# A two-layer mixture-of-experts network: permanent routing tables, fewer routing products, and fetches moved into the last expert block

## The chip, the cores and the metric

The kernel runs on one core of one Trainium2 chip. The metric is the device time of one execution in microseconds; the kernel before has a median of 3048.8 us over 3 runs (3047.92 to 3056.55). Its five engines are named as the profile names them: PE (TensorE, matmuls; PEld its weight loads), DVE (VectorE), ACT (ScalarE), POOL (GpSimd) and SP (SyncE, which here only issues transfers).

## The reference, cut to what matters

512 tokens of width 1024 in float32 pass a first network of two layers and then a second one of two layers. Each layer of the first network is a mixer (a gated delta rule in layer 0, a sparse attention in layer 1) with a layer norm behind it, and a mixture of experts with a layer norm behind it:

```python
h = layer_norm(DEEPNORM_ALPHA * h + mix, ln_mix_g[layer], ln_mix_b[layer])
ffn = hier_moe(h, ...)     # per token: best of 4 groups, best 2 of its 4 experts
h = layer_norm(DEEPNORM_ALPHA * h + ffn, ln_ffn_g[layer], ln_ffn_b[layer])
# hier_moe: logits of 4 groups and of 16 experts; y = sum of 2 weighted
#           expert outputs (silu(x @ wg) * (x @ wu)) @ wd, hidden width 256
```

The change concerns only what lies between a mixer's output projection and the first projection of what follows, once in each of the two layers.

## The kernel before, in words

**Arithmetic.** A matrix product in float32 is done as three products of rounded parts: x and w are each split into a high part (ACT copies with rounding) and a low part (DVE or POOL subtracts), and PE adds high x high, low x high and high x low. In the code `wf` is a weight tile as loaded, `wh` its high part, `wl` its low part. Tokens are in four tiles of 128 (`TT = 4`), the width in eight slices of 128 (`KT = 8`, `HALF = 4`).

**Stages.** The program is a row of stages. At the end of each (`Stage.__exit__`, L72) semaphores are cleared and all engines meet in a barrier, so nothing crosses it that is not issued by hand in an earlier stage. Each engine has its own order of work, written out in the code; a wait holds all that stands behind it on that engine. Four stages matter here, in this order, in each layer:

1. *Output norm* (`stage_out_norm`, tiles `gwo_...` in layer 0 and `nwo_...` in layer 1). PE computes the second half of the output projection tile by tile (L1082), between them the routing logits of an earlier tile (`Logits.pe`, L1118: per tile 8 slices x 3 products of 20 columns) and the transposes of the normed tile (`Turn.pe`, L964). ACT and DVE split the transposed tile (L970, L975), and the logits of a tile wait for that (`lo_done`). At the end DVE adds the bias (`Logits.take`, L1124). `LayerNorm` works on DVE: statistics, `centre` (L1004) with the gain, `finish` (L1016) with the shift; the root between them is on ACT.
2. *Experts* (`stage_experts`, tiles `exp_...` and `rt_...`). SP first loads four small constant tables (`Route.load`: descending numbers, thresholds, places, a counter `iota_b`), then a counter of 256 columns (L1473), then the weights of blocks 0 and 1 (L1395, L1400). DVE works out from the logits which expert and which slot each token gets (`Route.slots`), waiting for all four tables behind its second step; PE counts the tokens per expert in between (`Route.pe`, four accumulating products of 16 columns at L1298; in the trace each is two instructions). Tokens are thus sorted into blocks of 128 per expert. PE gathers the tokens of a pair of blocks by a product with a 0/1 matrix (`choose` on DVE L1627, L1633 builds it; L1511), multiplies with the gate and up weights (L1527, `body`), transposes the hidden tile (L1537) and multiplies with the down weights (L1548); DVE multiplies the two hidden halves (`hid`, L1653), ACT does the silu and copies y, SP stores each block's y to memory (L1479). `pairs` runs blocks 0 and 1, then a hardware loop from a number read from a table (`last_pair`, L1449), then the last pair. Here both layers have 16 blocks. DVE splits half of each block's low parts, POOL the other half (L1414). Ahead of `pairs` DVE computes the mixing weights (`Route.weights`) and scales the four tiles of h (L1674). When the last y is stored, POOL fetches for each tile of tokens the rows of its two experts by index (L1614, into expert weight tiles that are free by then, `rows_back`), and DVE adds them to h (L1685).
3. *Norm behind the experts* (`stage_ffn_norm`, tiles `ffn_ln_...`). SP loads gain and shift (L991, L992), in layer 1 also the gain of the second network's norm, then the first weights of the next projection; ACT and POOL split the first half of them in this stage (`hi_first` at t = 1, L153; `lo_first`, L159). DVE norms tile by tile, PE transposes, ACT and DVE split.
4. The next projection, in layer 0 behind a short stage that builds bias tables.

Where a line number is a helper's (L153, L159, L964), the tile's name tells the stage.

## Time and profile before

| | |
|---|---|
| median of 3 runs | 3048.8 us (3047.92 to 3056.55) |
| the profiled execution, its own time | 3048.18 us |
| its span in the profile | 3046.4 us |
| PE busy | 2520.5 us (83% of the span) |
| DVE, ACT, POOL busy | 1244.7, 970.6, 756.1 us |
| mean granted clock of PE | 0.898 |
| transfers | 304.42 MB, 100 GB/s in the mean |

How to read it: the profile is of one execution. The time outside the span is 1.8 us. Times in rows are counted from the span's start. A timeline row gives start, duration, engine, line, operation, written tile <- read tiles, shapes and the number of merged instructions; in brackets the idle time of the engine before it and what ended it. A row of a window gives its length, then busy time (number of instructions) of PE, PEld, DVE, ACT and POOL, the granted clock of PE as a share of 2.4 GHz (1.00 is the upper of its two levels, 0.50 the lower), the busy share of the 16 DMA engines and GB/s. Busy shares say little by themselves: what counts is which wait ends last in each stage.

### The profile page before, as it was taken

The page shows a single profiled execution, that of the slowest core. Times are in us where ns is not written, and L with a number is a line of the kernel's source. Part 1 is how long each engine was busy: PE and PEld are TensorE (multiplying, and loading weights), DVE is VectorE, ACT ScalarE, POOL GpSimd, SP SyncE. Part 2 cuts the span into 40 slices and gives each one's busy share as a digit, 9 for nine tenths or more (in the row PEclk, how much of TensorE's full clock was granted, in tenths as well). Part 3 has the DMA queues.
Part 4 walks back from the last instruction along what each step waited for, and adds up shares of the span by engine and source line. Part 5 has one row for each costly group of instructions (what it writes and reads, how often), then busy time and mean ns, then how long its engine had stood idle before and what let it go on. Part 6 is the DMA issues. An engine that isn't in the chain of part 4 may idle for free. (4 is left out here: it accounts for less than half of the span.)

```text
span 3046.4 us, 34677 instructions
## 1 busy us (share of the span) xinstructions
PE 2520.5 (83%) x13130; PEld 1983.7 (65%) x13130; DVE 1244.7 (41%) x2600; ACT 970.6 (32%) x1543; POOL 756.1 (25%) x214
## 2 busy tenths in 40 slices
PE   6996888687992987997998378986999878896998
PEld 4774777576771775666775346765887737675886
DVE  3524555435444306765543544142022262222122
ACT  2332112223441114762443224242222332332222
POOL 2430000212441320010333211323443202234441
PEclk9997999888995996997999688997999989997999
DMA  4350000016873233112686411212322202223221
GB/s 111 102 208 7 1 1 1 28 53 209 282 260 115 85 85 134 50 56 85 209 278 204 160 36 52 88 56 70 127 97 78 87 28 69 71 70 100 97 83 63
DMA packets 220925, 304.42 MB, mean 100 GB/s; under 512 B 52226, under 2 KB 139796, under 8 KB 220772
## 3 DMA queue, kind: packets, MB, share of 16 engines
q1 hardware_dynamic: 218484, 294.18, 29.6%
q0 software_dynamic: 2304, 8.39, 0.8%
q8 instruction: 89, 1.46, 0.2%
q14 instruction: 48, 0.39, 0.0%
HBM read 270.97 MB, written 31.56 MB: 99 GB/s over the span
## 5 line engine op out<-in xcount | busy, mean ns | idle before, releaser
L159 POOL TENSOR_TENSOR branch_weights_wl<-branch_weights_wf,branch_weights_wh 128x2048 fp32r<-128x2048 f32 (+1 forms) x66 | 300.0, 4546 | 779.3 <-ACT branch_weights_wh L153 779.3
L1414 POOL TENSOR_TENSOR rt_wl<-rt_wf,rt_wh 128x2048 fp32r<-128x2048 f32 x32 | 167.1, 5223 | 396.9 <-ACT rt_wh L1410 256.3
L153 ACT ACTIVATE branch_weights_wh<-branch_weights_wf 128x2048 fp32r<-128x2048 f32 (+1 forms) x66 | 125.0, 1894 | 411.5 <-PE bprojc_acc L201 129.2
L201 PE MATMUL merge_acc<-xh,branch_weights_wh 128*128 128x512 f32 x384 | 151.1, 393 | 18.3 <-PEq L72 18.3
L201 PE MATMUL merge_acc<-xl,branch_weights_wh 128*128 128x512 f32 x384 | 150.7, 393 | 0.0
L201 PE MATMUL merge_acc<-xh,branch_weights_wl 128*128 128x512 f32 x384 | 150.5, 392 | 0.0
L159 POOL TENSOR_TENSOR nsa_weights_wl<-nsa_weights_wf,nsa_weights_wh 128x2048 fp32r<-128x2048 f32 x13 | 59.8, 4604 | 295.7 <-ACT nsa_weights_wh L153 295.7
L1410 ACT ACTIVATE rt_wh<-rt_wf 128x2048 fp32r<-128x2048 f32 x64 | 122.0, 1907 | 3.8 <-DMA rt_wf<-moe_w_up 3.8
L1548 PE MATMUL exp_ps_y<-rt_wf,exp_ht 128*128 128x512 f32 x256 | 117.7, 603 | 3.7 <-ACT exp_ht L1589 3.7
L1527 PE MATMUL exp_ps_gu<-rt_wh,exp_xh 128*128 128x512 f32 x256 | 113.2, 442 | 0.0
L159 POOL TENSOR_TENSOR in_weights_wl<-in_weights_wf,in_weights_wh 128x2048 fp32r<-128x2048 f32 x16 | 75.0, 4686 | 127.1 <-ACT in_weights_wh L153 109.5
L201 PE MATMUL gproj_acc<-xh,in_weights_wh 128*128 128x512 f32 x256 | 100.4, 392 | 4.2 <-POOL in_weights_wl L159 4.2
L2707 DVE TENSOR_TENSOR merge_prod<-merge_gate,merge_b 128x512 f32<-128x512 f32 x32 | 21.9, 684 | 196.8 <-PE merge_b L2651 196.8
L1527 PE MATMUL exp_ps_gu<-rt_wl,exp_xh 128*128 128x512 f32 x256 | 100.9, 394 | 0.0
L1527 PE MATMUL exp_ps_gu<-rt_wh,exp_xl 128*128 128x512 f32 x256 | 100.9, 394 | 0.0
L201 PE MATMUL gproj_acc<-xh,in_weights_wl 128*128 128x512 f32 x256 | 99.7, 389 | 0.0
L201 PE MATMUL gproj_acc<-xl,in_weights_wh 128*128 128x512 f32 x256 | 99.6, 389 | 0.0
L201 PEld LDWEIGHTS merge_acc<-xh,branch_weights_wh 128*128 128x128 f32 x384 | 73.0, 190 | 33.9 <-issue 18.7
L1511 PE MATMUL exp_ps_xh<-exp_pick,xh 128*128 128x256 f32 x512 | 78.6, 299 | 15.5 <-DVE exp_pick L1633 12.3
L1643 DVE CAST exp_xl<-exp_ps_xl 128x1024 fp32r<-128x1024 f32 x32 | 39.2, 1224 | 127.0 <-PE exp_ps_gu L1527 103.9
L625 PE MATMUL gchunk_ps<-gchunk_tm,gchunk_m 128*128 128x128 f32 x384 | 61.5, 312 | 32.7 <-DVE gchunk_m L749 32.7
L805 POOL MEMSET gscan_state<- 128x1024 f32 x1 | 1.0, 951 | 334.7 <-POOLq L72 334.7
(598 smaller groups left out, 6529.6 us busy)
## 6 DMA issues: line engine op xcount, KB each, us to landing
branch_weights_wf<-w_in SPq DMA_DIRECT2D x56, 1024.0 KB, 4.9
rt_wf<-moe_w_gate SPq DMA_DIRECT2D x64, 512.0 KB, 6.6
rt_wf<-moe_w_up SPq DMA_DIRECT2D x64, 512.0 KB, 7.7
rt_wf<-moe_w_down SPq DMA_DIRECT2D x32, 1024.0 KB, 6.0
in_weights_wf<-gdn_w_in SPq DMA_DIRECT2D x16, 1024.0 KB, 5.5
moe_rows<-exp_y SPq DMA_DIRECT2D x32, 512.0 KB, 3.0
moe_rows<-gproj_zeros SPq DMA_DIRECT2D x1, 12288.0 KB, 35.5
merge_bwf<-w_branch SPq DMA_DIRECT2D x12, 1024.0 KB, 5.0
```

The costliest lines, as they stand in the source:

```text
L153: act.activation(self.h[u][:, :, 0:self.cols(b)], self.s.f[u][:, :, 0:self.cols(b)], ACT.Copy).then_inc(self.s.hi_ready, 1)
L159: pool.tensor_tensor(self.l[u][:, :, 0:self.cols(b)], self.s.f[u][:, :, 0:self.cols(b)], self.h[u][:, :, 0:self.cols(b)].bitcast(F32), ALU ...
L201: mm = pe.matmul(self.acc[:, s, 0:cols], lhs[:, P * s:P * s + P], rhs, start=(u == 0 and k == 0 and n == 0), stop=(u == 1 and k == HALF - ...
L625: mm = pe.matmul(bank(i, 3, c), b["m"][:, c, :], b["tm"][:, c, :], start=True, stop=True)
L805: pool.memset(state[:], 0.0).then_inc(zeroed, 1)
L1410: act.activation(self.h[b][u][:], self.f[b][u][:], ACT.Copy).then_inc(self.hi_ready[u], 1)
L1414: eng.tensor_tensor(self.l[b][u][:], self.f[b][u][:], self.h[b][u][:].bitcast(F32), ALU.subtract).then_inc(self.lo_ready[u], 1)
L1511: mm = pe.matmul(dst[:, kk // 2, 2 * P * (kk % 2):2 * P * (kk % 2) + 2 * P], src[:, t, P * k:P * k + P], pick[:, t, :], start=(t == 0), st ...
L1527: mm = pe.matmul(ps_gu[:, 0, :], x[:, HALF * u + k, P * b:P * b + P], w[b][u][:, k, :], start=(u == 0 and k == 0 and m == 0), stop=(u == 1 ...
L1548: mm = pe.matmul(ps_y[:, c, :], ht[:, k, :], down[:, k, c, :], start=(k == 0), stop=(k == 1))
L1643: dve.tensor_copy(xl[:, HALF * v:HALF * v + HALF, :].rearrange("p k n -> p (k n)"), ps_xl[:].rearrange("p b n -> p (b n)")).then_inc(xl_ou ...
L2707: dve.tensor_tensor(prod[:, f % 2, :], gate[:, f, :], ps_b[:, f, :], ALU.mult).then_inc(b_out, 1)
```

## The change

- The three tables of the routing (`desc`, `thr`, `place`) become permanent tiles, loaded once in the first stage behind the first weights. The fourth, `iota_b`, is gone: the block list reads the counter of 256 columns, which the experts need anyway and still load as the first transfer of their stage.
- The logits: high and low part of the router weights stand side by side (`lwp`), so that one product of 40 columns takes the place of two of 20: 16 instead of 24 products per tile. `take` adds the two halves with one more DVE instruction. On PE the last tile's transposes come ahead of the third tile's logits.
- The count per expert: one product of 64 columns in place of four of 16, and a DVE reduction over the four tiles behind it.
- The mixing weights and the scaling of h move on DVE from ahead of block 0's multiply to behind the first pair.
- The expert stage and the norm behind it share a region of memory with the weight slots of the next projection: `wf0_0`, `wf0_1`, `wh0`, `wl0` of the experts are these slots. SP loads the next projection's first weights when the last blocks no longer need them, ahead of the last two stores; ACT takes their first high part in the last block, ahead of its wait for that block's products, and POOL the low part behind its loop.
- Gain and shift of the norm behind the experts are loaded on SP behind the last stores, the gain into the comparison tile `eq0`, the shift into `y` once y is stored. The gathered rows go to other weight tiles.

```diff
...
                 sp.dma_start(g.neg_below[:], a["c_neg_below"]).then_inc(ld, 16)
                 sp.dma_start(g.striu[:], a["c_striu"]).then_inc(ld, 16)
                 nxt.load_first(sp)
+                sp.dma_start(g.desc[:], rows_of(a["c_desc"], 0, N_GRP)).then_inc(consts_in, 16)
+                sp.dma_start(g.thr[:], rows_of(a["c_thr"], 0, TT - 1)).then_inc(consts_in, 16)
+                sp.dma_start(g.place[:], bass.AP(a["c_place"].tensor, a["c_place"].offset,
+                                                 [[0, P], [N_EXP, 2], [1, N_EXP]])).then_inc(consts_in, 16)
+                sp.wait_ge(consts_in, 16 * 3)
 
             @block.gpsimd
...
         h = self.g.h[:, t, :]
         dve.wait_ge(self.stat, stats)
         dve.bn_aggr(self.mv[:, t, :], self.parts[:, t, :, :].rearrange("p a b -> p (a b)")).then_inc(self.agg, 1)
-        if t == 0:
+        if t == 0 and not self.early:
...
             pe.wait_ge(self.turn.lo_done, 2 * t + half + 1)
             for k in range(HALF * half, HALF * half + HALF):
-                for m, (x, w) in enumerate(((self.g.xh, self.wh), (self.g.xl, self.wh), (self.g.xh, self.wl))):
-                    mm = pe.matmul(self.acc[:, 0, self.n * t:self.n * t + self.n], x[:, k, P * t:P * t + P], w[:, k, :],
-                                   start=(k == 0 and m == 0), stop=(k == KT - 1 and m == 2))
+                cols = slice(P * t, P * t + P)
+                pe.matmul(self.acc[:, 0, 2 * self.n * t:2 * self.n * (t + 1)], self.g.xh[:, k, cols], self.wp[:, k, :],
+                          start=(k == 0), stop=False)
+                mm = pe.matmul(self.acc[:, 0, 2 * self.n * t:2 * self.n * t + self.n], self.g.xl[:, k, cols],
+                               self.wp[:, k, 0:self.n], start=False, stop=(k == KT - 1))
         mm.then_inc(self.done, 1)
 
     def take(self, dve, out):
         dve.wait_ge(self.done, TT)
-        dve.tensor_tensor(out[:], self.acc[:, 0, 0:TT * self.n].rearrange("p (t n) -> p t n", t=TT),
-                          self.bias[:].unsqueeze(1).to_broadcast([P, TT, self.n]), ALU.add).then_inc(self.taken, 1)
+        acc = self.acc[:, 0, 0:2 * TT * self.n].rearrange("p (t n) -> p t n", t=TT)
+        dve.tensor_tensor(out[:], acc[:, :, 0:self.n],
+                          self.bias[:].unsqueeze(1).to_broadcast([P, TT, self.n]), ALU.add).then_inc(self.biased, 1)
+        dve.wait_ge(self.biased, 1)
+        dve.tensor_tensor(out[:], out[:], acc[:, :, self.n:], ALU.add).then_inc(self.taken, 1)
 
...
                     if t:
                         pe.wait_ge(norm.done, t)
                         turn.pe(pe, t - 1)
-                logits.pe(pe, TT - 2)
                 pe.wait_ge(norm.done, TT)
                 turn.pe(pe, TT - 1)
+                logits.pe(pe, TT - 2)
                 logits.pe(pe, TT - 1)
...
 
 
...
     with Stage(nc, name) as st:
-        norm = LayerNorm(g, st, gain, shift)
+        norm = LayerNorm(g, st, None, None, vectors)
         pre = PreNorm(g, st, pre_gain) if pre_gain else None
         last = pre or norm
         turn = Turn(g, st, pre.xn if pre else g.h)
         with nc.Block() as block:
             @block.sync
             def _(sp):
-                norm.load(sp)
                 if pre:
                     pre.load(sp)
-                nxt.load_first(sp)
 
             @block.tensor
...
                 for t in range(TT):
                     pe.wait_ge(last.done, t + 1)
                     turn.pe(pe, t)
-
-            @block.gpsimd
-            def _(pool):
-                nxt.lo_first(pool)
 
             @block.scalar
...
                     if pre:
                         act.wait_ge(norm.done, t + 1)
                         pre.root(act, t)
-                    if t == 1:
-                        nxt.hi_first(act)
...
             pe.matmul(self.ps[:, 0, 16 * (t + 1):64], self.g.ones[:],
                       oh[:, t:t + 1, :].to_broadcast([P, TT - 1 - t, N_EXP]), start=False, stop=(t == TT - 2))
-        for t in range(TT):
-            mm = pe.matmul(self.ps[:, 0, 64:80], self.g.ones[:], oh[:, t, :], start=(t == 0), stop=(t == TT - 1))
-        mm.then_inc(self.counted, 1)
+        pe.matmul(self.ps[:, 0, 64:128], self.g.ones[:], oh[:].rearrange("p t e -> p (t e)"),
+                  start=True, stop=True).then_inc(self.counted, 1)
 
...
         for n, onehot in enumerate((self.oh1, self.oh2)):
             link(pair(self.f[:, n], onehot))
         dve.wait_ge(self.counted, 1)
-        link(dve.tensor_tensor(self.over[:], self.ps[:, 0, 64:80].unsqueeze(2).to_broadcast([P, N_EXP, TT - 1]),
+        link(dve.tensor_reduce(self.cnt[:], self.ps[:, 0, 64:128].rearrange("p (t e) -> p e t", t=TT), AX.X, ALU.add))
+        link(dve.tensor_tensor(self.over[:], self.cnt[:].unsqueeze(2).to_broadcast([P, N_EXP, TT - 1]),
...
         self.link = link
 
     def tables(self, dve):
-        link, tabf, iota_b, n = self.link, self.tabf, self.iota_b, MAX_BLOCKS
-        link(dve.tensor_tensor(self.le[:], self.incl[0:1, :].unsqueeze(1).to_broadcast([1, MORE_BLOCKS, N_EXP]),
-                               iota_b[:, 0:MORE_BLOCKS, :], ALU.is_le))
-        dve.tensor_copy(tabf[:, 0:N_EXP], iota_b[0:1, 0:N_EXP, 0])
...
 
 
-    def __init__(self, region, a, layer):
-        self.f = [[region.sb(f"wf{b}_{u}", [P, HALF, 512]) for u in range(3)] for b in range(2)]
-        self.h = [[region.sb(f"wh{b}_{u}", [P, HALF, 512], F32R) for u in range(2)] for b in range(2)]
-        self.l = [[region.sb(f"wl{b}_{u}", [P, HALF, 512], F32R) for u in range(2)] for b in range(2)]
+    def __init__(self, region, slots, a, layer):
+        unit = [P, HALF, 512]
+        self.f = [[*slots.f, region.sb("wf0_2", unit)], [region.sb(f"wf1_{u}", unit) for u in range(3)]]
+        self.h = [slots.h, [region.sb(f"wh1_{u}", unit, F32R) for u in range(2)]]
...
+        pick, eq0, y = st.sb("pick", [P, TT, 2 * P], F32R), rt.eq0, rt.y
         xh, xl = st.sb("xh", [P, KT, 2 * P], F32R), st.sb("xl", [P, KT, 2 * P], F32R)
         act_g, hid = st.sb("act_g", [P, HID]), st.sb("hid", [P, HID])
...
             return eng.value_load(rt.table[0:1, MAX_BLOCKS:MAX_BLOCKS + 1], min_val=N_EXP // 2 - 1,
                                   max_val=MAX_BLOCKS // 2 - 1)
 
-        def pairs(eng, body):
+        def pairs(eng, body, after_first=None):
             body(0, 0, 0, False)
             body(0, 1, 1, False)
+            if after_first:
+                after_first()
             end = last_pair(eng)
...
             return end
 
 
-        rows_back = [x[:].rearrange("p (k a) n -> p k (a n)", k=2) for x in (*ws.f[0], ws.f[1][0])]
+        rows_back = [x[:].rearrange("p (k a) n -> p k (a n)", k=2) for x in (ws.f[0][2], *ws.f[1])]
...
                         sp.wait_ge(y_done, i - 1)
                         ws.load_down(sp, b, e)
+                for u in range(2):
+                    sp.wait_ge(ws.lo_ready[u], end * 2 + 1)
+                nxt.load_first(sp)
                 for b in range(2):
                     store(end * 2 + b)
+                sp.wait_ge(picked, end + 2)
+                sp.dma_start(rt.vectors[0], rows_of(a["ln_ffn_g"], layer * D, D)).then_inc(ln_in, 16)
+                sp.wait_ge(y_stored, end * 32 + 32)
+                sp.dma_start(rt.vectors[1], rows_of(a["ln_ffn_b"], layer * D, D)).then_inc(ln_in, 16)
+                sp.wait_ge(ln_in, 32)
...
                         hi_next(j, b, 0)
                     if b == 1 and not last:
                         x_hi(j + 1, 0)
+                    if last:
+                        act.wait_ge(unit0_used, i)
+                        nxt.hi_first(act)
...
                 with pool.Fori(1, end + 1) as j:
                     for b in range(2):
                         ws.lo(pool, b, 1, j * 2 + (b + 1))
+                nxt.lo_first(pool)
...
                 x_lo(0, 1)
                 route.tables(dve)
                 choose(1)
-                route.weights(dve)
-                for t in range(TT):
-                    ins = dve.tensor_scalar(g.h[:, t, :], g.h[:, t, :], ALPHA, None, ALU.mult)
-                ins.then_inc(scaled, 1)
-                end = pairs(dve, body)
+
+                def scale():
+                    route.weights(dve)
+                    for t in range(TT):
+                        ins = dve.tensor_scalar(g.h[:, t, :], g.h[:, t, :], ALPHA, None, ALU.mult)
+                    ins.then_inc(scaled, 1)
+                end = pairs(dve, body, scale)
...
+def moe_layer(g, a, layer, slots, nxt, pre_gain):
     nc = g.nc
     with Stage(nc, f"rt{layer}") as region:
         rt = Globals()
-        rt.weights = ExpertWeights(region, a, layer)
+        rt.weights = ExpertWeights(region, slots, a, layer)
 
         def psb(name, shape, dt=F32):
             return region.sb(name, shape, dt)
         rt.slot, rt.slot_i, rt.weight = psb("slot", [P, 2, TT]), psb("slot_i", [P, 2, TT], I32), psb("weight", [P, 2, TT])
         rt.table = psb("table", [1, MAX_BLOCKS + 1], I32)
         rt.hh, rt.hl = g.xh[:].rearrange("p (t a) n -> p t (a n)", t=TT), g.xl[:].rearrange("p (t a) n -> p t (a n)", t=TT)
-        stage_experts(g, f"exp{layer}", a, layer, rt)
-
-
-def ffn_norm(g, a, layer, nxt, pre_gain):
-    stage_ffn_norm(g, f"ffn_ln{layer}", (a["ln_ffn_g"], layer * D), (a["ln_ffn_b"], layer * D), nxt, pre_gain)
+        rt.eq0, rt.y = psb("eq0", [P, TT, 2 * P]), psb("y", [P, D])
+        rt.vectors = rt.eq0[:].rearrange("p t n -> p (t n)"), rt.y[:]
+        stage_experts(g, f"exp{layer}", a, layer, rt, nxt)
+        stage_ffn_norm(g, f"ffn_ln{layer}", rt.vectors, pre_gain)
...
             slots = WeightSlots(region)
             blocks = nsa_blocks(a)
             run = WeightRun(slots, len(blocks), lambda b: blocks[b][0], parts=2)
             out_run = WeightRun(slots, 2, lambda b: column_block(a["nsa_w_o"][0], 0, b * 512))
-            ffn_norm(g, a, 0, run, None)
+            moe_layer(g, a, 0, slots, run, None)
             stage_tables(g, a)
             nsa_layer(g, a, run, out_run)
-        moe_layer(g, a, 1)
         with Stage(nc, "branch_weights") as region:
             slots = WeightSlots(region)
             runs = [layer_runs(slots, a, layer) for layer in range(2)]
-            ffn_norm(g, a, 1, runs[0]["b"], (a["pre_g_2"], 0))
+            moe_layer(g, a, 1, slots, runs[0]["b"], (a["pre_g_2"], 0))
```

## Rows read from the trace of the kernel before

**Rows 1.** Stage windows: us; busy by engine; granted clock; DMA share; GB/s.
```profile
640.00:665.00 25.00, 23.97 (x143) 20.91 (x141) 19.17 (x29) 4.32 (x10) 0.00 (x0) 1.00 0.00 1
757.00:920.00 163.00, 159.29 (x788) 121.06 (x787) 76.44 (x91) 77.60 (x75) 62.06 (x13) 1.00 0.79 261
920.00:947.00 27.00, 3.55 (x8) 1.29 (x8) 10.43 (x9) 1.02 (x1) 8.15 (x8) 0.66 0.49 175
...
932.00:934.00 2.00, 0.00 (x0) 0.00 (x0) 0.00 (x0) 0.00 (x0) 1.70 (x2) 0.50 0.97 334
```

**Rows 2.** Timeline of the output norm tail, layer 0: start, us, engine, line.
```profile
663.57 1.28 DVE L1016 SCALAR_TENSOR_TENSOR h<-h,gwo_inv,gwo_lnb 128x1024 f32<-128x1024 f32 x1
...
670.55 1.97 PE L964 MATMUL gwo_turn<-ident,h 128*128 128x128 f32 x8
673.08 0.39 PE L1118 MATMUL gwo_logits<-gwo_lwh,xh 128*128 128x20 f32 x1 [0.56 <-DVE xl L975]
...
678.41 0.24 DVE L1124 TENSOR_TENSOR logits<-gwo_logits,gwo_lbias 128x80 f32<-128x80 f32 x1 [4.53 <-PE gwo_logits L1118]
```

**Rows 3.** Waits for the constant (both layers), then the timeline of the routing in layer 0.
```profile
  DMA exp_iota_b<-c_iota_b: 8.0, 2
...
684.91 0.26 DVE L1321 TENSOR_REDUCE exp_el<-exp_t 128x16 f32<-128x64 f32 x1
...
689.70 1.87 PE L1298 MATMUL exp_ps_t<-exp_oh,ones 128*128 128x16 f32 x8
...
691.68 0.21 DVE L1342 TENSOR_TENSOR exp_over<-exp_ps_t,exp_thr 128x48 f32<-128x48 f32 x1 [3.36 <-PE exp_ps_t L1298]
...
702.76 6.56 POOL L1414 TENSOR_TENSOR rt_wl<-rt_wf,rt_wh 128x2048 fp32r<-128x2048 f32 x1 [68.90 <-DVE xl L1665]
```

**Rows 4.** Timelines, first pairs, layers 0 and 1; then two lines by form.
```profile
717.00 1.10 PE L1511 MATMUL exp_ps_xl<-exp_pick,xl 128*128 128x256 f32 x8
...
723.99 0.69 PE L1537 MATMUL exp_ps_t<-ident,exp_hid 128*128 128x128 f32 x2 [5.89 <-DVE exp_hid L1653]
...
730.57 0.80 PE L1527 MATMUL exp_ps_gu<-rt_wh,exp_xh 128*128 128x512 f32 x1
...
738.46 0.38 PE L1537 MATMUL exp_ps_t<-ident,exp_hid 128*128 128x128 f32 x2
...
743.60 0.79 PE L1527 MATMUL exp_ps_gu<-rt_wh,exp_xh 128*128 128x512 f32 x1
...
750.22 0.42 DVE L1653 TENSOR_TENSOR exp_hid<-exp_act_g,exp_ps_gu 128x256 f32<-128x256 f32 x1 [3.16 <-ACT exp_act_g L1583]
...
752.06 5.15 POOL L1414 TENSOR_TENSOR rt_wl<-rt_wf,rt_wh 128x2048 fp32r<-128x2048 f32 x1 [7.86 <-ACT rt_wh L1410]
...
1459.04 1.11 PE L1511 MATMUL exp_ps_xl<-exp_pick,xl 128*128 128x256 f32 x8
...
1473.59 0.80 PE L1527 MATMUL exp_ps_gu<-rt_wh,exp_xh 128*128 128x512 f32 x1
...
L1674 DVE TENSOR_SCALAR h<-h x8: 684/692/4986, 716.8 to 1460.7; 128x1024 f32<-128x1024 f32 x8
...
L1449 DVEq TENSOR_LOAD <-rt_table x2: 757/866/974, 746.9 to 1489.9; - x2
```

**Rows 5.** Layer 0, end of the experts and the norm behind; then waits of both layers.
```profile
902.20 0.38 SPq L1400 DMA_DIRECT2D rt_wf<-moe_w_down  x1
...
912.53 1.03 ACT L1595 ACTIVATE exp_y<-exp_ps_y 128x1024 f32<-128x1024 f32 x1 [4.03 <-PE exp_ps_y L1548]
...
934.85 8.05 DVE L1685 SCALAR_TENSOR_TENSOR h<-rt_wf,rt_weight,h 128x1024 f32<-128x1024 f32 x6 [7.16 <-DMA rt_wf<-moe_rows,rt_slot_i]
...
962.68 2.93 DVE L1004 SCALAR_TENSOR_TENSOR h<-h,ffn_ln_mv,ffn_ln_lng 128x1024 f32<-128x1024 f32 x1
...
  DMA ffn_ln_lnb<-ln_ffn_b: 8.3, 2
...
ffn_ln_lnb<-ln_ffn_b SPq DMA_DIRECT2D x2, 512.0 KB, 5.3
```

65 lines of the change are left out of this document (30 added, 35 removed).

## The prediction

> **What bounds the kernel now.** I read the table of stage windows first, then the timelines of TensorE (PE), VectorE (DVE), ScalarE and GpSimd around each place that the diff touches, then the two tables of waits for the tiles concerned. The windows show two regimes. In the output projection with its norm and in the loop over pairs of expert blocks PE is busy nearly all the time at a granted clock of 1.00, and there only fewer PE instructions would help [rows 1]. Between them lie stretches in which PE does little and one chain of small steps, mostly on DVE, sets the end: the tail of the output norm, the routing at the start of the expert stage, the gather of the results and the norm behind it [rows 1]. Such a chain runs twice, once per layer. Almost every edit of this change lies on one of these chains, so that a wait taken from it is time taken from the kernel, unless the next thing is late too. That is checked part by part.
>
> **Output norm (two stages).** Behind the last norm of tile 3 (DVE, ends at 663.57 + 1.28 = 664.85) PE finishes 24 small products of tile 2, transposes tile 3 from 670.55, waits for its halves and does the 24 products of tile 3, and DVE adds the bias at 678.41: 13.56 us [rows 2]. Cold, a product comes every 0.214 us ((1.87 - 0.37) / 7 in the group of eight [rows 3]). The new order transposes tile 3 first, then does 16 products of tile 2 and 16 of tile 3. The wait for tile 3's split halves (2.5 us from the first transpose to the first product [rows 2]) is covered by tile 2's 16 x 0.214 = 3.4 us. New length: 8 transposes x 0.214 = 1.7, 32 x 0.214 = 6.85, and 0.2 until the last lands: 8.8, so 4.8 us less. Is a product of 40 columns dearer than one of 20? The trace has none; the eight of 16 columns keep the same pace as the 24 of 20 (678.41 - 673.08 = 5.3 us with the landing [rows 2]), which is the pace of the weight load and not of the columns, so I take it as free, with 0 and, if the time went by columns, all that packing brings (rival B) as the ends. DVE gets one more add of its kind (0.24 with its hand-over 0.27 [rows 2]). While PE is the bound, at clock 1.00 [rows 1], tile 0's products stand ahead of the last block: 8 fewer x 0.107 = 0.9. Sum: 4.8 - 0.3 + 0.9 = 5.4 a stage, **10.7 us** in two. If the clock stayed high in the tail it would be up to 3.4 us more a stage.
>
> **Constants.** DVE waits 8.0 us in two waits for the last routing constant [rows 3]. With the tables on the chip since the first stage both waits go. Next to be late would be the 256-column counter tile: it is now the first transfer of the stage and is needed only behind the whole routing, later than the count at 691.68 [rows 3]. The expert weights are issued four transfers earlier on SP's queue, and they were not what mattered: GpSimd's first split was released by DVE, not by a weight [rows 3]. **8.0 us**. The three loads in the first stage stand behind the weights on SP, and that stage ends with GpSimd's split of those weights, so I cost them at nothing; without that cover it would be one landing, some 3 us.
>
> **Counting.** Eight PE instructions become two: 6 x 0.214 = 1.3 us from DVE's wait of 3.36 [rows 3]. DVE gets a reduction of 64 elements to 16, for which the trace has its like: 0.26, with the hand-over 0.3 [rows 3]. 1.0 a layer, **2.0 us**. The tables written for the block list are as many instructions as before.
>
> **The scaling of h moved behind the first pair.** Here is the largest term. After block 0 PE wants to transpose the hidden tile at 718.1 and gets it at 723.99, with 5.89 us idle, because DVE scales the four tiles of h first. Body 1 starts at 730.57. For the next block the same distance, transposes to body, is 738.46 to 743.60, 5.14 us [rows 4]. Without the wait body 1 starts at 718.1 + 5.14 = 723.2: 7.3 us earlier; part of that is the clock, which no longer drops. In layer 1: 1459.04 + 1.11 + 5.14 = 1465.3 against 1473.59, 8.3 us [rows 4]. Together 15.6. The work now stands before hid of block 2. DVE is idle there for 3.16 us until 750.22; the weights of the mix (4 small steps, 0.8) and four scalings at the median of 0.69 end at 747.06 + 0.8 + 2.8 = 750.7. The multiply (0.42) then ends at 751.1, and PE asks for it at 743.60 + 7.89 = 751.5 [rows 4]. So it just fits. The register load ahead of the loop (0.87 [rows 4]) is overlapped or not: 0 to 0.9 a layer, I take 0.4. **14.8 us**. This cover is thin: what it costs if GpSimd takes part is rival A.
>
> **Norm behind the experts.** DVE waits 8.3 us in two waits for the norm's scale and offset [rows 5]: gone. The offset now lands in the y tile, the scale in the comparison tile, both issued after the last store and long there before the norm. GpSimd's split of the next weights moves into the last block; in the norm it stretched one DVE step from 1.28 to 2.93 us [rows 5, 2], the same in layer 1: 3.3 us. In layer 1 the other gain vector is still loaded in the norm, now as the first of its queue; it is needed only when the first tile has been normed. **11.6 us**.
>
> **The early fetch itself.** On SP the next weights (2 MB, in layer 1 less) stand behind the last expert load (902.20) and before the last two stores; ScalarE splits them before it waits for block 15's products, behind the y copy that ends at 913.6 [rows 5]. That leaves over 10 us for 2 MB, and ScalarE is free between that copy and the end of block 15's products (it was idle for 4.03 us ahead of the copy). GpSimd has nothing else. I cost this at nothing. The scale and offset (512 KB each as replicated; the offset took 5.3 us to land [rows 5]) run just before and in the gather, in which the transfers are at 0.97 of the engines and 334 GB/s [rows 1]. One of them costs 0.52 MB / 334 GB/s = 1.6 us if DVE, which waits 7.16 us for the first gathered rows [rows 5], gets these later. Ends: 0 (both done before) and 3.1 a layer (both ahead). I take the one that is issued when the last store has landed: 1.6 a layer, **-3.2 us**. The Trainium skill, DMA: Bandwidth & Descriptors, section "Issuing engines are not separate DMA queues", says that transfers issued by SP and by GpSimd run on the same 16 DMA engines and interleave; by it the two share and the loss falls near my value, by separate queues it would be nothing. No row here shows both at once.
>
> **Sum.** 10.7 + 8.0 + 2.0 + 14.8 + 11.6 - 3.2 = 43.9 us. The profiled execution took 3048.2 us (span 3046.4), which gives 3004.3; the median of the three runs is 0.6 us above it, which gives **3005 us**, 1.4% less. A measurement of this kernel can tell about 0.3%, 9 us, from no change.
>
> **Rivals.** A, the moved scaling meets GpSimd. GpSimd's next split starts at 752.06, and the last scaling is to end at 750.7: 1.4 us of room [rows 4]. In its old place one of the scalings took 4.99 us instead of 0.69 [rows 4], beside such a split. If that happens again, DVE is free only at 752.06 + 5.15 = 757.2, hid comes at 757.6 and PE waits 6.1 us where it now has none, and loses up to 1.5 us to the clock as in the first pair: 7.6 a layer, so 3020. For it: the room is thin, the rows show the effect. Against: all steps before it move together with PE. The Trainium skill, SBUF — State Buffer, section "Who interferes with whom", says that a DVE instruction in a two-port mode, such as a scaling, and a GpSimd instruction exclude each other and that the later one waits for the whole of the other; the trace agrees in its 4.99 us, and by that rule it hangs on who starts first.
>
> B, products cost by columns. Then 16 products of a tile cost what 24 did, only the new order stays: 1.7 + 48 x 0.214 = 12.0 and 0.2 for 13.56: 1.4 less the added 0.3. The stages bring 2.2 instead of 10.7: 3013. Against: the flat pace in [rows 3].
>
> C, it does not do what it says: behind each wait removed another ends at nearly the same time (counter tile, first weights, gathered rows), and the scaling gives back what it gained. Then 3040 to 3049. Against: the releasers in [rows 3].
>
> D, slower. The pair loop keeps the transfers 0.79 busy at 261 GB/s [rows 1]. The old stall in the first pair gave the weight loads 7 us of lead; without it, and with prefetches and stores behind the same SP queue, the loads might fall behind PE in each of the 14 later pairs. It decides from the point at which the transfer share in the loop reaches 1.00. To end at over 3058 it has to lose the 43.9 and 9 more, 53 / 14 = 3.8 us a pair. That needs 30 us of transfers for what now takes 0.79 x 26 = 20.6. Nothing in the change adds bytes to the loop.
>
> **Chances.** Forecast 0.72 (2996 to 3013 with the unknown terms at their ends: no loss in the gather and one tail at high clock, -3.2 and -5; full loss, a late register load and a slower tail, +3, +1 and +4), A 0.12 (3020), B 0.08 (3013), a mixture that gives back more, 3021 to 3039, 0.03, C 0.03, D 0.02. Faster by over 0.3%: 0.72 + 0.12 + 0.08 + 0.03 = 0.95; the same 0.03; slower 0.02. The range for 8 in 10 is 2996 to 3020.
>
> **What would show it.** In the changed kernel: no DVE idle time on a constant at the start of the experts; two PE instructions in the count; 16 logit products a tile, the last behind a transpose that starts right after the norm; the transposes of block 0 without a wait on hid and body 1 some 5 us behind them; block 2's hid without lateness and all eight scalings near 0.7 us; no wait on scale or offset, no DVE step of 2.9 us in the norm; the first gathered row at most 3 us later than now, counted from the last store. The forecast is wrong if a wait of several us stands before block 2's transposes (A), if the 40-column products come at twice the pace (B), if the pair loop is longer than 26 us (D), or if ScalarE waits for the next weights in the last block.

## The result, and the profile after the change

The changed kernel took 3017.7 us (median of 4 runs, 3011.97 to 3023.2) against 3050.7 for the kernel before on the same chip: a ratio of 0.9889, 95% interval 0.9864 to 0.9914, so 1.1% faster, some 34 us. The profiled execution took 3011.97 us (span 3010.2), 36.2 us less than the span of before. Forecast were 43.9 us less and 3005 us, with a range of 2996 to 3020. The time lies in the range, 12.7 us above the forecast. All times and ratios below are of undisturbed executions: one of the ten of experiment e11 took 6118.2 us at a mean granted clock of 0.387 and is left out.

First the windows that answer [rows 1] (columns as there), in the changed kernel, layer 0: output projection, pair loop, gather.

```profile
640.00:665.00 25.00, 23.17 (x130) 19.62 (x129) 19.54 (x29) 4.33 (x10) 0.00 (x0) 1.00 0.00 1
751.00:903.00 152.00, 148.77 (x728) 111.94 (x726) 72.43 (x88) 72.25 (x69) 63.69 (x13) 1.00 0.84 277
903.00:931.00 28.00, 3.90 (x10) 1.44 (x8) 10.18 (x9) 1.44 (x3) 8.57 (x9) 0.65 0.58 206
```

The regimes are the same; the share of the transfers in the pair loop is 0.84, not 1.00. Now the timeline from the last norm step to the count, for [rows 2, 3]:

```profile
663.51 1.28 DVE L1021 SCALAR_TENSOR_TENSOR h<-h,gwo_inv,gwo_lnb 128x1024 f32<-128x1024 f32 x1
...
664.85 1.51 PE L969 MATMUL gwo_turn<-ident,h 128*128 128x128 f32 x8 [1.83 <-DVE h L1021]
...
672.19 0.37 PE L1126 MATMUL gwo_logits<-gwo_lwp,xl 128*128 128x20 f32 x1
672.41 0.38 PE L1124 MATMUL gwo_logits<-gwo_lwp,xh 128*128 128x40 f32 x1
672.62 0.37 PE L1126 MATMUL gwo_logits<-gwo_lwp,xl 128*128 128x20 f32 x1
...
673.02 0.24 DVE L1133 TENSOR_TENSOR logits<-gwo_logits,gwo_lbias 128x80 f32<-128x80 f32 x1 [5.31 <-PE gwo_logits L1126]
673.30 0.24 DVE L1136 TENSOR_TENSOR logits<-logits,gwo_logits 128x80 f32<-128x80 f32 x1
...
680.89 0.67 PE L1292 MATMUL exp_ps_t<-exp_oh,ones 128*128 128x64 f32 x2
...
681.67 0.22 DVE L1335 TENSOR_REDUCE exp_cnt<-exp_ps_t 128x16 f32<-128x64 f32 x1 [2.16 <-PE exp_ps_t L1292]
```

The last transposes start as the norm step ends. At the lower clock level products with 40 and with 20 columns both follow at 0.21 us, as the products of 20 did: rival B is out. DVE's wait for the count is 2.16 us instead of 3.36, and nothing waits for a constant any more. The first pair and the moved scaling, for [rows 4] (timeline, layer 0; the last line is L1685 by form over both layers, whose three durations are ns, shortest/median/longest):

```profile
709.25 0.38 PE L1542 MATMUL exp_ps_t<-ident,exp_hid 128*128 128x128 f32 x2
...
714.40 0.79 PE L1532 MATMUL exp_ps_gu<-rt_wh,exp_xh 128*128 128x512 f32 x1
...
735.90 5.16 POOL L1410 TENSOR_TENSOR rt_wl<-rt_wf,rt_wh 128x2048 fp32r<-128x2048 f32 x1 [7.86 <-ACT rt_wh L1406]
...
L1685 DVE TENSOR_SCALAR h<-h x8: 684/685/694, 731.6 to 1451.4; 128x1024 f32<-128x1024 f32 x8
```

The transposes have no wait, and body 1 starts 714.40 - 709.25 = 5.15 us behind them (forecast 5.14). All eight scalings take 0.68 to 0.69 us, and the one of 4.99 us is gone: rival A is out, GpSimd's split comes after them. The end of the experts and the norm, for [rows 5]:

```profile
897.28 1.91 ACT L153 ACTIVATE nsa_weights_wh<-nsa_weights_wf 128x2048 fp32r<-128x2048 f32 x1
899.26 4.55 POOL L159 TENSOR_TENSOR nsa_weights_wl<-nsa_weights_wf,nsa_weights_wh 128x2048 fp32r<-128x2048 f32 x1 [1.95 <-ACT nsa_weights_wh L153]
...
907.49 1.02 ACT L1603 ACTIVATE rt_y<-exp_ps_y 128x1024 f32<-128x1024 f32 x1 [3.87 <-PE exp_ps_y L1553]
909.16 0.37 SPq L1494 DMA_DIRECT2D rt_eq<-ln_ffn_g  x1
911.66 0.34 SPq L1496 DMA_DIRECT2D rt_y<-ln_ffn_b  x1
...
919.89 10.17 DVE L1696 SCALAR_TENSOR_TENSOR h<-rt_wf,rt_weight,h 128x1024 f32<-128x1024 f32 x8 [8.07 <-DMA rt_wf<-moe_rows,rt_slot_i]
...
931.00 1.28 DVE L1000 BATCH_NORM_STATS2 ffn_ln_stats<-h 128x6 f32<-128x512 f32 x2 [0.94 <-PEq L72]
...
932.57 1.29 DVE L1009 SCALAR_TENSOR_TENSOR h<-h,ffn_ln_mv,rt_eq 128x1024 f32<-128x1024 f32 x1
```

ScalarE and GpSimd split the next weights in the last block, and the norm's first centring takes 1.29 us without a wait. The split on ScalarE (897.28) stands there without a wait, so the next weights were in time. The gathered rows come later than before: DVE waits 8.07 us for the first, where it waited 7.16 [rows 5].

Laid end to end, from one start of a DVE step to the next, the stretches that the change touches are these (us, layer 0 / layer 1; e1 is the first experiment below):

| stretch | before | changed | e1 | gain, changed | forecast |
|---|---|---|---|---|---|
| last norm step to bias add | 14.84 / 14.73 | 9.51 / 9.98 | 8.90 / 8.73 | 10.1 | 9.6 |
| to the slot copy (routing) | 16.22 / 16.72 | 11.85 / 11.84 | 11.84 / 11.85 | 9.3 | 9.4 |
| to hid of block 1 | 42.55 / 44.62 | 36.15 / 35.54 | 35.41 / 35.58 | 15.5 | 14.8 |
| to hid of block 15 | 181.29 / 182.96 | 181.26 / 182.95 | 183.15 / 183.15 | 0.0 | 0 |
| to the first step of the norm | 28.75 / 28.63 | 28.72 / 28.34 | 28.76 / 28.32 | 0.3 | -3.2 |
| to the last low half of the norm | 27.68 / 35.89 | 21.52 / 29.99 | 21.51 / 30.00 | 12.1 | 11.6 |

The first row of e1 is not better by its placement: the granted clock falls later in its tail (mean over the tail 0.66 and 0.68, in the changed kernel 0.62 and 0.54, before 0.57 in both layers). The gains of the changed kernel add up to 47.2 us, 3.3 more than the whole forecast, which has another 1.8 for tile 0's products, ahead of the first stretch. So every part came out near its value or better, and still the kernel gained only 36. The rest is lost where nothing was edited. The same two DVE steps, the first copy behind the last expert norm and a late step of the last output projection, in the kernel before:

```profile
1742.98 0.59 DVE L2329 COPY br_mla<-bprojb_acc 128x416 f32<-128x416 f32 x1 [14.60 <-PE bprojb_acc L201]
...
3017.75 0.69 DVE L2794 TENSOR_TENSOR bout_y<-bout_acc,bout_gain 128x512 f32<-128x512 f32 x1 [2.02 <-ACT bout_junk L2771]
```

and in the changed kernel:

```profile
1695.59 0.59 DVE L2340 COPY br_mla<-bprojb_acc 128x416 f32<-128x416 f32 x1 [14.63 <-PE bprojb_acc L201]
...
2981.23 0.69 DVE L2805 TENSOR_TENSOR bout_y<-bout_acc,bout_gain 128x512 f32<-128x512 f32 x1 [2.11 <-ACT bout_junk L2782]
```

The lead is 47.39 us at the first and 36.52 at the last: 10.9 us are given back in the branch layers, in small steps over long stretches in which PE is busy without a break. There each product takes longer. Timeline of PE in the merge, before:

```profile
2142.50 0.39 PE L201 MATMUL merge_acc<-xh,branch_weights_wh 128*128 128x512 f32 x1
2142.72 0.39 PE L201 MATMUL merge_acc<-xl,branch_weights_wh 128*128 128x512 f32 x1
2142.95 0.39 PE L201 MATMUL merge_acc<-xh,branch_weights_wl 128*128 128x512 f32 x1
2143.18 0.39 PE L201 MATMUL merge_acc<-xh,branch_weights_wh 128*128 128x512 f32 x1
```

and after:

```profile
2102.28 0.40 PE L201 MATMUL merge_acc<-xh,branch_weights_wh 128*128 128x512 f32 x1
2102.51 0.40 PE L201 MATMUL merge_acc<-xl,branch_weights_wh 128*128 128x512 f32 x1
2102.74 0.40 PE L201 MATMUL merge_acc<-xh,branch_weights_wl 128*128 128x512 f32 x1
2102.98 0.40 PE L201 MATMUL merge_acc<-xh,branch_weights_wh 128*128 128x512 f32 x1
```

Three products take 0.68 us before and 0.70 after, at the same granted clock of 1.00. Of the two operands behind the arrow the first is the moving one (512 columns pass through PE), the second the stationary one (loaded as weights, 128 columns).

### The profile page after: what moved, and what is told of

The parts are those of the page before. It is cut to its first block and busy times, and to the rows that moved or that the text cites. A ratio compares the mean times of both kernels' runs of the same rounds, so it can differ in the third digit from the quotient of the medians.

```text
span 3010.2 us, 34531 instructions
## 1 busy us (share of the span) xinstructions
PE 2517.3 (84%) x13054; PEld 1966.3 (65%) x13054; DVE 1235.6 (41%) x2604; ACT 969.9 (32%) x1543; POOL 758.7 (25%) x214
## 5 line engine op out<-in xcount | busy, mean ns | idle before, releaser
L1410 POOL TENSOR_TENSOR rt_wl<-rt_wf,rt_wh 128x2048 fp32r<-128x2048 f32 x16 | 82.6, 5163 | 129.2 <-ACT rt_wh L1406 129.2
L201 PEld LDWEIGHTS merge_acc<-xh,branch_weights_wl 128*128 128x128 f32 x384 | 73.2, 191 | 17.3
L201 PEld LDWEIGHTS merge_acc<-xl,branch_weights_wh 128*128 128x128 f32 x384 | 73.6, 192 | 16.4
L1516 PEld LDWEIGHTS exp_ps_xh<-exp_pick,xh 128*128 128x128 f32 x512 | 69.7, 197 | 20.1 <-DVE exp_pick L1642 14.2
L201 PE MATMUL bprojc_acc<-xh,branch_weights_wh 128*128 128x512 f32 x192 | 76.1, 396 | 5.9 <-PEq L72 5.9
```

Of the source, the lines that this page charges most:

```text
L201: mm = pe.matmul(self.acc[:, s, 0:cols], lhs[:, P * s:P * s + P], rhs, start=(u == 0 and k == 0 and n == 0), stop=(u == 1 and k == HALF - ...
L1410: eng.tensor_tensor(self.l[b][u][:], self.f[b][u][:], self.h[b][u][:].bitcast(F32), ALU.subtract).then_inc(self.lo_ready[u], 1)
L1516: mm = pe.matmul(dst[:, kk // 2, 2 * P * (kk % 2):2 * P * (kk % 2) + 2 * P], src[:, t, P * k:P * k + P], pick[:, t, :], start=(t == 0), st ...
```

## The experiments

**What could slow products that nobody touched.** Theory "placement": the three tables that became permanent take 16, 12 and 128 B a partition, each rounded up to 32 B, together 192 B, and were put behind h, the activations xh and xl, and the small permanent tiles. So the activations stayed, and all that is allocated later, the weights of every stage among it, moved by 192 B. Before, the weights stood by the allocation order a multiple of 512 B behind xh, since the small tiles between them fill 512 B exactly. Rival "traffic": the moved fetches are to blame.

**e1 and e4, padding behind the tables.**

```diff
         g.desc, g.thr, g.place = sb("desc", [P, N_GRP]), sb("thr", [P, TT - 1]), sb("place", [P, 2, N_EXP])
+        sb("pad", [P, 16])
```

> The changed kernel with one more unused permanent tile of 64 B a partition behind the three tables, so that everything allocated after them starts 256 B later than before the change instead of 192 B (a multiple of 128 B again); nothing else differs. Theory placement (the three permanent tables moved all later tiles off a 128 B boundary, and each 512-column product of the split-weight stages is then spaced 229 to 233 ns instead of 226.7): the spacing returns to 226.7 in the projections, the merge and the output products, the stretch behind the second expert norm is about 1317 us as before the change instead of 1328, and the whole kernel gains 1.5 (input projection) + 1.1 + 1.5 + 1.2 + 10.8 = 16 us: span 2994, time 3001 if held against the median of the changed kernel, 2996 against its profiled run; ratio to before 0.983. Theory traffic (the loss comes from the moved fetches and code, not from addresses): nothing changes, 3012 to 3018, spacing 229 to 233.

For e4 there is `psb("pad", [P, 8])` ahead of rt.eq0 as well.

> The kernel of e1 and another 32 B of padding ahead of the expert stage's tiles, which start 96 B behind a 128 B boundary in the kernel before and in e1: its one-hot, activation and hidden tiles then start on a boundary too. Placement: the 768 gate and up products are spaced 226.7 instead of 233 ns, 4.8 us over both layers, and the gathers and down products may gain as much again; 4 to 9 us below e1, about 2993 against the median. Traffic: equal to e1 within 2 us.

**e2 and e3, the kernel before with nothing but an unused tile** behind the logits, `sb("pad", [P, 48])` (192 B) and `sb("pad", [P, 8])` (32 B).

> The kernel before with one unused permanent tile of 192 B a partition, so that every later tile lies where it lies in the changed kernel; nothing else differs. Placement: slower than the kernel before by about 16 us (3065), with 512-column products at 229 to 233 ns in gproj, nproj, the branch projections and merge, and 233 in gwo, nwo and bout. Traffic: 3049, spacing 226.7.

> The kernel before with one unused permanent tile of 32 B a partition. It asks at what distance the placement counts. If only the boundary of 64 B or less counts, products slow here at least as much as with 192 B (3065 or more); if 128 B counts, about the same 3065; if it is a matter of banks far apart rather than of the start within 128 B, 3049. Traffic: 3049.

Measured: e1 2997.5 us (ratio to before 0.9816, 0.9801 to 0.9832); e4 2993.4 (0.9801, 0.9785 to 0.9817); e2 3069.1 (1.0054, 1.0036 to 1.0072); e3 3078.7 (1.0085, 1.0069 to 1.0101). Mean distance between the starts of successive products in ns (all distances of 0.20 to 0.26 us within a tile; 165 to 1136 of them in a cell), of these and of two later experiments:

| tile written (moving / stationary) | before | changed | e1 | e2 | e3 | e11 | e12 |
|---|---|---|---|---|---|---|---|
| gproj (xh / weights) | 227.0 | 229.0 | 226.9 | 229.0 | 233.4 | 227.0 | 226.9 |
| gwo (weights / xh) | 227.4 | 233.3 | 227.4 | 233.3 | 233.3 | 227.4 | 227.3 |
| nproj | 226.8 | 229.8 | 226.7 | 229.8 | 233.3 | 226.7 | 226.8 |
| bprojc | 226.7 | 230.1 | 226.7 | 231.2 | 233.3 | 226.7 | 226.7 |
| bproja | 226.7 | 230.3 | 226.9 | 230.3 | 233.3 | 226.9 | 226.7 |
| merge (xh / weights) | 226.7 | 229.4 | 226.7 | 229.1 | 233.4 | 226.7 | 226.7 |
| merge_b (both operands lie behind the tables) | 226.7 | 227.6 | 226.7 | 227.6 | 227.1 | 226.7 | 226.7 |
| bout (weights / xh) | 227.1 | 233.3 | 227.1 | 233.3 | 233.3 | 227.0 | 226.9 |

Placement stands and traffic falls: an unused tile alone makes the kernel before 16 us slower (0.0054 x 3049), with nearly the changed kernel's distances, and 64 B of padding take the loss away. By the ratios e1 is 0.0073 or 22 us faster than the changed kernel, by the two profiled spans 12 us; 16 were expected.

Three rows hold products of both kinds: nproj, bproja and bprojc. By kind the changed kernel has 228.9 to 229.0 ns in them with xh moving and 233.3 to 233.4 with the weights moving.

The changed kernel's excess, product by product, is 16.4 us: 768 x 2.0 ns in gproj, 192 x 5.9 in gwo, 480 x 3.0 in nproj, 192 x 6.4 in nwo; then in the branch layers 192 x 1.8 (bprojb), 768 x 3.4, 576 x 3.6, 1152 x 2.7, 576 x 0.9 and 384 x 6.2, together 11.0 where 10.9 were seen lost. e4 is not told apart from e1 by its time. Its gate and up products come at 228.5 ns instead of 233.2, but a block takes 12.97 us instead of 13.03, 0.9 us a layer over 14 blocks, where 4.8 in all were expected. The distance expected was 226.7: by the allocation order the operands of these products stand 256 B off a multiple of 512 B in e4, as the weights do in e1, and yet they are slower than the weights' products there.

The table has one row that doesn't fit the words of e1: in e3 merge_b kept its pace, though both its operands stood off the boundary.

```profile
2200.92 0.39 PE L2651 MATMUL merge_b<-br_yh,merge_bwh 128*128 128x512 f32 x1
...
2201.60 0.39 PE L2651 MATMUL merge_b<-br_yh,merge_bwh 128*128 128x512 f32 x1
```

0.68 us for three, in the kernel in which the merge beside it takes 0.70:

```profile
2156.47 0.40 PE L201 MATMUL merge_acc<-xh,branch_weights_wh 128*128 128x512 f32 x1
...
2157.17 0.40 PE L201 MATMUL merge_acc<-xh,branch_weights_wh 128*128 128x512 f32 x1
```

So perhaps not where an operand starts, but how the two lie to each other.

**e11 and e12, everything moved together.** e11 is the kernel before with 32 B ahead of h:

```diff
+        sb("pad", [P, 8])
         g.h = sb("h", [P, TT, D])
```

> The kernel before with one unused tile of 32 B a partition ahead of the first permanent tile, so that every tile, the activations too, lies 32 B later; in e3 the activations stayed and only what follows them moved, and there the one product whose two operands had both moved (merge_b) kept 227.1 ns. Theory boundary (an operand that doesn't start on 128 B slows a product): every 512-column product takes 233 ns, 3075 to 3080 as e3. Theory relative place (what counts is how the moving and the stationary operand lie to each other): 226.7 ns, about 3052 as the kernel before.

e12 is the changed kernel with the line of its three tables put ahead of g.h.

> The changed kernel with its three permanent tables allocated ahead of h and the activations instead of behind them; no padding. All large tiles then lie 192 B later together. Theory boundary: spacing 229 to 233 ns or worse, 3017 to 3025. Theory relative place: 226.7 ns and the time of e1, 2997.5 (ratio 0.9816).

Measured: e11 3054.7 us (ratio 1.0005, 0.9991 to 1.002), e12 2999.0 (0.9827, 0.9809 to 0.9846), both with all distances of the table back at 226.7 to 227.4. The merge in e11, where every operand starts 32 B off the boundary:

```profile
2144.81 0.39 PE L201 MATMUL merge_acc<-xh,branch_weights_wh 128*128 128x512 f32 x1
...
2145.49 0.39 PE L201 MATMUL merge_acc<-xh,branch_weights_wh 128*128 128x512 f32 x1
```

The boundary theory falls: the same 32 B cost 26 us behind the activations (e3) and nothing that the runs can tell ahead of them (e11). The relative place stands as what decides in these stages; e4 shows that the distance alone does not give the pace of every product.

**The parts of the change, one at a time.** e5, e6, e7 and e10 undo one part of e1; e8 and e9 do one part alone in the kernel before.

e5, scaling ahead of the pairs:

```diff
-                end = pairs(dve, body, scale)
+                scale()
+                end = pairs(dve, body)
```

> The changed kernel at the old placement (e1), with the four scalings and the routing weights put back ahead of the first pair of experts. Prediction's step: 14.8 us are lost again (7.4 a layer, between the first and the second block of the first pair), so 3012 against e1's 2997.5. Rival (the moved scaling is paid for elsewhere, by the split weights or the second gather): 7.6 a layer comes back and nothing is lost, 2997.

3015.1 us (0.9880, 0.9863 to 0.9896), 0.0064 or 20 us above e1. From the slot copy to hid of block 1 it takes 43.18 / 43.94 us instead of 35.41 / 35.58: 16.1 us. The old wait is back, in both layers:

```profile
713.20 0.69 PE L1542 MATMUL exp_ps_t<-ident,exp_hid 128*128 128x128 f32 x2 [5.89 <-DVE exp_hid L1662]
...
1439.70 0.69 PE L1542 MATMUL exp_ps_t<-ident,exp_hid 128*128 128x128 f32 x2 [5.89 <-DVE exp_hid L1662]
```

The other 5 us of its profiled span (3019.2 against 2998.0) lie in unchanged stages, above all here, in the same stretch of attention, which ran at a lower granted clock (windows, e5, then e1):

```profile
1795.00:1825.00 30.00, 28.17 (x143) 17.82 (x141) 16.65 (x65) 14.72 (x41) 0.00 (x0) 0.76 0.11 36
```

```profile
1775.00:1805.00 30.00, 26.89 (x173) 16.91 (x172) 19.17 (x72) 17.57 (x52) 0.00 (x0) 0.94 0.11 36
```

e6, scale and offset loaded by the norm stage (the two fetches of SP in the expert stage taken out, norm.load(sp) put back):

> e1, with the norm's scale and offset fetched by the norm stage itself, as before the change, into the same tiles. Prediction's step: the two waits for them come back (8.3 us over both layers) and the contention with the stores and the gather goes (3.2): 5.1 slower than e1, 3002.6. Rival, contention costs nothing because the barrier hides it: 8.3 slower, 3006. In the trace: the time from the slot copy to the first added row is 7.3 us again instead of 8.2, and the wait for the offset ahead of the first centring 3.7 us or more.

3002.6 us (0.9835, 0.9818 to 0.9852), 0.0019 or 6 us above e1. The norm takes 24.87 / 33.53 instead of 21.51 / 30.00, 6.9 more; the stretch ahead of it 28.28 / 28.34 instead of 28.76 / 28.32, 0.5 less. That the two fetches delay the gathered rows is shown too: with them gone from the gather, DVE waits 7.13 us for the first row, close to the 7.16 of before, where e1 has 7.90; but it waits again between the rows.

```profile
917.97 2.61 DVE L1692 SCALAR_TENSOR_TENSOR h<-rt_wf,rt_weight,h 128x1024 f32<-128x1024 f32 x2 [7.13 <-DMA rt_wf<-moe_rows,rt_slot_i]
```

The wait for the offset, which the change took away, is this:

```profile
934.82 1.28 DVE L1009 SCALAR_TENSOR_TENSOR h<-h,ffn_ln_mv,rt_eq 128x1024 f32<-128x1024 f32 x1 [3.40 <-DMA rt_y<-ln_ffn_b]
```

e7, next weights fetched and split in the norm (nxt.load_first, hi_first and lo_first put back there):

> e1, with the next projection's first weights fetched and split during the norm stage, as before the change. Prediction's step: only the DVE step that the split on GpSimd stretched comes back (3.3 us over both layers): 3001. Rival 1, the fetch behind the experts was worth nothing: 2997.5. Rival 2, without the vectors' fetch ahead of it the first weights now land earlier in the norm, so the split meets another step: the loss is still between 0 and 5.

3006.3 us (0.9855, 0.9837 to 0.9873). By its runs 12 us above e1, by the place only 3.9: the norm takes 23.16 / 32.20, and the profiled span is 4.2 longer. The step beside GpSimd's split is stretched again:

```profile
941.38 2.92 DVE L1009 SCALAR_TENSOR_TENSOR h<-h,ffn_ln_mv,rt_eq 128x1024 f32<-128x1024 f32 x1
```

The 8 us between the two are not explained; the two intervals are 5 us wide at each side.

e8, the kernel before with the changed logits (product of 40 columns, second add, new order) alone:

> The kernel before with the change to the logits alone (products of 40 columns, two adds, the last transposes ahead of the third tile's products); the placement of all that counts is that of the kernel before. Prediction's step: 10.7 us faster than before, 5.3 a layer, all of it between the last norm step and the logits: 3042.5 of 3053.2. Rival, part of the 5 us seen between those two points in the changed kernel came from elsewhere (the clock, the fetches): 2 to 6 us faster.

3039.4 us (0.9956, 0.9939 to 0.9973), 13 us faster than before. The tail takes 8.83 / 9.72 instead of 14.84 / 14.73: 11.0. In its profiled execution (span 3040.8, only 5.6 less) 4.0 of layer 0 are given back in the first pair (44.69 against 42.55) and in the pair loop (183.16 against 181.29). That is not a cost of the edit: e11, in which nothing is edited, has 44.66 and 183.16 in the same place. In both the granted clock is lower there, 0.79 against 0.82 over the first pair, and at the end of the pair loop as follows; the first line is e8, the second the kernel before:

```profile
900.00:915.00 15.00, 12.70 (x41) 7.80 (x40) 2.88 (x4) 3.74 (x5) 5.13 (x1) 0.89 0.35 126
903.00:918.00 15.00, 12.70 (x47) 8.20 (x46) 2.98 (x4) 3.85 (x5) 5.17 (x1) 1.00 0.35 128
```

e1's longer 183.15 in the table of stretches goes with the same fall (0.88 in 885:899).

e10, only the order undone in e1:

```diff
+                logits.pe(pe, TT - 2)
                 pe.wait_ge(norm.done, TT)
                 turn.pe(pe, TT - 1)
-                logits.pe(pe, TT - 2)
                 logits.pe(pe, TT - 1)
```

> The changed kernel at the old placement (e1) with the logits of the third tile again ahead of the last transposes, and the products still of 40 columns. It splits the 5 us of the tail: by the order 16 products at 0.11 to 0.21 us and the wait for the low part of the third tile (0.7 us) stand ahead of the last transposes, of which 16 products come back behind: 3 to 5 us a layer would be lost, so nearly all of the gain, 3003 to 3007, if the order is what counts. Rival, the gain is that of the fewer products (16 instead of 24 a tile): under 1.5 us a layer lost, 2998 to 3000.

3002.9 us (0.9839, 0.9823 to 0.9856), by its runs 7 us above e1, within 5 us either way, which by itself would fit the first expectation. By the place it is less: the tail takes 10.63 / 10.42 instead of 8.90 / 8.73, 1.7 a layer, between my two expectations and near the rival. The clock falls at about the same point in both (mean over the tail 0.64 and 0.65, in e1 0.66 and 0.68). So the order is worth 1.7 of the 6 us that e1's tail gained. The other 4.2 are the fewer products and some 0.6 of clock: the changed kernel, with e1's code and a mean clock of 0.62, gained 5.3 in layer 0 and not 5.9. With the old order and fewer products the last transposes start late, but no longer by much, and the wait of 0.56 us ahead of tile 3's products is back:

```profile
669.23 1.97 PE L969 MATMUL gwo_turn<-ident,h 128*128 128x128 f32 x8
...
671.76 0.40 PE L1124 MATMUL gwo_logits<-gwo_lwp,xh 128*128 128x40 f32 x1 [0.56 <-DVE xl L980]
```

e9, the kernel before with permanent tables and 64 B of padding:

> The kernel before with the three routing tables permanent, as in the change, and 64 B of padding behind them, so that everything later starts on the boundary it had; the fourth table (the counts) is still fetched by the expert stage. Prediction's step: the two waits go, 8.0 us faster over both layers, 3044 of 3052. Rival, the wait comes back at a later step for the fourth table or for the first expert weights: 0 to 4 us faster. Theory placement: no 512-column product changes its spacing (226.7).

3040.7 us (0.9964, 0.9952 to 0.9977), 11 us faster than before. In place it is 7.9: the routing takes 12.52 / 12.49 us instead of 16.22 / 16.72. The fourth table is not waited for, so for the constants rival C is out too. Another 3.2 us of its profiled span were gained in the chunk stage, which no edit touches and which ran at a granted clock of 0.91; the first line is e9, the second the kernel before:

```profile
280.00:520.00 240.00, 187.33 (x1446) 176.91 (x1445) 142.46 (x266) 47.29 (x111) 0.00 (x0) 0.91 0.00 1
```

```profile
280.00:520.00 240.00, 187.21 (x1421) 177.07 (x1420) 139.87 (x261) 47.27 (x111) 0.00 (x0) 0.89 0.00 1
```

## Why the prediction was right, and where it wasn't

The direction and the terms were right; the sum had one term too few. That the range held it is in part luck: from the forecast 43.9 us the missing term took 16.4, the parts brought 5.1 more than forecast and the unedited stages 3.6 (below), which leaves the 36.2 of the profiled execution.

- **Output norm**, forecast 4.8 a stage in the tail (5.4 with tile 0's products and the second add). The tail gained 5.3 and 4.8, and 5.9 and 6.0 in e1, where the clock fell later. Free columns: right. I had not split the gain between order and products; the products carry most of it (e10).
- **Constants and counting**, 8.0 + 2.0, less 0.6 for the second add. Measured 9.3 together, 7.9 of it the constants (e9).
- **Scaling moved**, 14.8. Measured 15.5, and 16.1 by undoing it (e5). The register load was hidden or within this.
- **Norm behind the experts**, 8.3 for the waits and 3.3 for the stretched step. Measured 12.1 together; undone one at a time 6.9 (e6) and 3.9 (e7).
- **The early fetch**, -3.2. Mis-sized: 0 to -0.5. The mechanism is there: DVE waits 8.07 us for the first gathered row instead of 7.16 [rows 5], and the small copy behind the last store, which releases the gather, comes 0.3 later. Without the two fetches (e6) the wait is 7.13 again. Yet DVE then adds all rows without a further wait, where it had waited in between, and the barrier behind is 0.94 us instead of 1.39. I had priced the first row and not the last. The Trainium skill, DMA: Bandwidth & Descriptors, section "Issuing engines are not separate DMA queues", by which the transfers of SP and of GpSimd share the engines, agrees with the later first row.
- **The step that failed**: "with the tables on the chip since the first stage both waits go", to which I set only their three loads, at nothing. The loads do cost next to nothing: the first product of the first projection starts at 30.99 us instead of 30.87, in the other runs that have the loads at 31.1 to 32.5, in those without them at 31.1 to 31.6. Making a tile permanent also moves every tile allocated behind it. That cost 16.4 us by the distances and 16 by e2. I took the time of each unchanged product from the kernel before without asking whether its operands stay where they are.
- **What is left over.** The gains of 47.2 less 16.4 would be 30.8, and the profiled execution gained 36.2, its runs 34. The difference of 5.4 lies in the first network: by the distances gproj, gwo, nproj and nwo should have cost that much, yet the lead grew by 0.1 us ahead of the first stretch and by 0.1 between the stretches of the two layers. Up to 1.8 are tile 0's products; the other 3.6 were won in stages with a varying clock. In the output stage of layer 1, for one, from one add of `nwo_acc` into h to the next (1390.42 to 1401.05 before, 1370.30 to 1378.53 after) the lead grew by 2.4 us. The first line is before, the second after:

```profile
1390.40:1401.10 10.70, 10.70 (x58) 9.55 (x59) 5.59 (x9) 1.49 (x3) 0.00 (x0) 0.84 0.00 0
1370.30:1378.50 8.20, 8.20 (x50) 7.12 (x49) 5.43 (x8) 1.39 (x3) 0.00 (x0) 1.00 0.00 0
```

Eight products fewer, 0.11 us apart at that clock, are 0.9 of the 2.4; the rest goes with the clock.
- **Rivals.** A and B fell to the rows above, C to them and to the time. D fell too: a pair takes some 26.04 us as before, with the transfers at 0.84.

At the old placement the sum could be held against the whole: e1's profiled span is 48.4 us below that of before, forecast 43.9, and its runs 1.8% (56 us, 51 to 61). The profiled execution of before is 5.0 us below the median of that comparison (3053.2) and that of e1 2.4 above its own, hence the two figures. The stretches of e1 gained 47.7, so 8 of the 56 us are not located, and the forecast of 43.9 lies below the interval.

## What to carry to other kernels

Before pricing an edit that allocates or frees a lasting tile, look at what lies behind it in memory: operands of the busiest engine that keep their distance to each other keep their pace, and others may not. Put new permanent tiles ahead of all large ones, or pad them so that the distance to the activations stays a multiple of 256 B; here that is worth as much as the largest part of the change. And compare the distance of starts of the same product in both traces before looking for a cause in the stages that were edited. Where one execution differs from the next by several us in stages with a varying clock, read a term of a few us from its own stretch, not from the total, and look at the clock of that stretch in both.

## What the hardware showed that was not expected

In the unedited projections and merges, products of 512 columns with split fp32 operands come every 226.7 ns at a granted clock of 1.00 when the tiles of the moving and the stationary operand start a multiple of 512 B apart (before) or 256 B off that (e1), 233.3 ns when one of them is shifted by 32 B, and 229 to 233.3 when it is shifted by 192 B, where it matters which of the two it is: 229.0 with the weights stationary (gproj), 233.3 with the weights moving (gwo, bout). The gate and up products, whose operands stand 224 B off by the allocation order, take 233 ns in every kernel but e4. Where both are shifted together nothing changes (e11, e12), or nearly nothing: merge_b is at 227.6 in the changed kernel, where the merge products that it alternates with are the slow ones. The Trainium skill, SBUF — State Buffer, section "Operand start alignment", asks only that an operand start at a multiple of its element size, which all of these do; of pace it says nothing. Why the distance counts was not tried, and neither was another dtype. Nor is it settled why the gate and up products stay at 228.5 ns in e4, at the distance at which e1's weights have 226.7.

The granted clock can also fall to its lower level for a moment where PE has no idle time (0.84 over the 10.70 us above, PE busy for all of them) and not do so at the same place of another execution. The loop of layer 0 that took 181.3 us had 1.00 at its end (kernel before, window shown under e8), and the one that took 183.2 had 0.89 (e8).
